# Attention stage: query weight pieces one after another, head norms woven between their halves, norm scratch in other tiles

## The chip, the cores and the metric

The kernel runs on one NeuronCore of one Trainium2 chip. The metric is the device time of one execution in microseconds (us). A core has TensorE (matmuls and transposes), VectorE (DVE in the rows), ScalarE (ACT), GpSimd (POOL) and SyncE (SP, which here only issues transfers). Each works through its own list of instructions in order, and they meet only at semaphores.

## The reference, cut to what matters

The whole reference is a sequence mixer with a table lookup, then a block of two layers over 256 tokens and 1024 channels: layer 0 pools and has a gated feed-forward net, layer 1 attends and has another one. The change lies in the attention of layer 1. Eight query heads of 128 share two key heads, and 256 context keys and values (worked out earlier) stand behind the 256 latent ones.

```python
q, k, v = split(h @ w_qkv)                 # 1024, 256, 256 columns
q = rmsnorm(q per head) * q_gain           # 8 heads
k = rmsnorm(k per head) * k_gain           # 2 key heads
q, k = rope(q), rope(k)                    # x * cos + swap(x) * sin
s = q @ keys.T * 128 ** -0.5
p = softmax(s)                             # fp32
o = p @ vals
x = x + gate * (o @ w_o)
```

## The kernel before, in words

**Layout.** Everything is kept turned, channels on the 128 partitions and the 256 tokens in the free dimension. `qT` holds the eight query heads, `kTt` the two key heads (latent columns 0 to 255, context 256 to 511).

**Weights in two parts.** A projection is worked out from a high and a low part of both operands, three matmuls of 256 columns instead of one (`mm3`, L1210). Weights come in pieces of 128x2048. For each piece ScalarE copies the high part (`hi_part`, L2547), VectorE (or GpSimd for pieces 34, 40 and 41) subtracts it to make the low part (`lo_part`, L1964), and only then can TensorE use it (`piece`, L1250). There are three places for the parts, so ScalarE may write piece n only when TensorE has used piece n - 3 (the wait on `p_u` n - 2). Piece 34 is the keys' weights, 35 the values', 36 to 39 the queries', two heads each, 40 to 43 the output projection's. A query piece is two halves (one head each) of 24 matmuls.

**Norm and rotation.** A `headnorm` n works on one key head (n = 0, 1; 256 columns) or on two query heads (n = 2 to 5; 512 columns). It is a chain that crosses the engines: ScalarE squares into a scratch tile (`square`), TensorE sums over the partitions by four matmuls with one column out ("hs"), ScalarE takes the root (`root`), VectorE the reciprocal, TensorE spreads it by four transposes ("hb"), VectorE multiplies head, gain and root ("hx"), TensorE swaps the rows for the rotation ("hr") while GpSimd multiplies by the cosine, VectorE multiplies the swapped rows by the sine ("ro"), and adds the two ("hn"). `scrs` has three sets of scratch, used in turn, so norm n's square waits for norm n - 3 to end.

**Order, written out by hand on each engine.** All engines' lists are Python loops and generators; `next(g)` puts down the next step of a generator.
- Pieces 34 and 35 (keys, values), then `colproj3` for pieces 36 and 37 (L1382).
- Norms 0 to 2 (two key heads and query heads 0 and 1), step by step over the three at once, with a step of `cond` after each. VectorE makes the low parts of pieces 38 and 39 only behind its third step of these norms (L2092), ScalarE the high parts behind its roots (L2623).
- `colproj3` for pieces 38 and 39, then the scores of head 0, norms 3 to 5 step by step with three more steps of `cond` and the scores of head 1.
- The loop over heads (L1400): transposes of the probabilities of head n, scores of head n + 2, output of head n - 1, and up to two steps of `cond`. `head_max` and `head_scale` are VectorE's side of the softmax, `exps` ScalarE's, `turned` the copies of the turned probabilities.

**cond** is `conditioning` (L788), which works out layer 1's modulation for the feed-forward net: 16 steps of four matmuls of 512 columns over eight 2 MB loads, some empty steps and two sums. Six steps lie ahead of the loop over heads, 18 calls in it.

**Loads.** SyncE issues 2 MB loads into three slots in turn; each waits until the slot's last content was used. In the attention the order is keys and values, two query loads, six `ada` loads for `cond`, the first half of the output weights, two `ada` loads, the second half, and then the feed-forward net's. A query load's slot is free when its second piece's low part is made (`split_done`), an `ada` load's when TensorE has used it.

**PSUM.** Eight banks, seven of them given out in turn by `take` (L651), which waits for the reader of what the bank held.

Of the kernel before, what the change touches and what calls it, by code (L numbers as in the profile page):

```python
# [96 lines left out]
def program(nc, a, out):  # L97
# [99 lines left out]
    def flat(ap):  # L197
        return ap.rearrange("p m n -> p (m n)")
# [166 lines left out]
    for l in range(2):  # L365
# [13 lines left out]
            (oT_[:, 0:512], oT_[:, 512:1024], oT_[:, 1024:1536]),  # L379
            (prT[:, 0:512], prT[:, 512:1024], prT[:, 1024:1536])]  # L380
# [267 lines left out]
    def _(pe):  # L648
# [693 lines left out]
        hn = [headnorm(0, kTt[:, 0, :], 1), headnorm(1, kTt[:, 1, :], 1)]  # L1342

        def colproj3(n0, name, reader, r0, per, base=None):

            for u in range(2):
                fresh = u == 0 and base is not None
                b = both_halves((name, u), reader, r0 + per * u, fresh)
                w = piece(n0 + u)
                for kk, i in rows_first(fresh):  # L1350
                    if fresh and i == 0:
                        row_there(base, kk)
                    k = mm3(b[i], both(w, 256 * kk + 128 * i, 128), both(ahx, 256 * kk, 256), kk == 0, kk == 7)
                k.then_inc(S["p_u"], 1)
# [26 lines left out]
        for q in range(2):  # L1381
            colproj3(36 + 2 * q, ("qp", q), "a_qT", 2 * q + 1, 1)  # L1382
            for u in range(2):
                hn.append(headnorm(2 + 2 * q + u, flat(qT[:, 4 * q + 2 * u:4 * q + 2 * u + 2, :]), 2))
            if q == 0:
                for _ in range(3):
                    for g in hn[0:3]:
                        next(g, None)
                    next(cond)
        hs = [head(h) for h in range(8)]  # L1390
        next(hs[0])
        rest = hn[3:]
        for s in range(3):
            for g in rest:
                next(g, None)
            if s == 1:
                next(hs[1])
            next(cond)
# [25 lines left out]
    def _(ve):  # L1424
# [638 lines left out]
        for u in range(2):  # L2063
            lo_part(36 + u, *half_piece(("q", 0), u))
        for _ in range(3):
            for g in hn[0:3]:
                next(g)
# [23 lines left out]

        for u in range(2):  # L2092
            lo_part(38 + u, *half_piece(("q", 1), u))
        for g in hn[0:3]:
            next(g)
        for step in range(4):
            for g in hn[3:6]:
                next(g)
            if step < 2:
                head_max(step)  # L2100
        for h in range(2):
            head_scale(h)
# [40 lines left out]
    def _(ac):  # L2143
# [459 lines left out]
        hi_part(37, *half_piece(("q", 0), 1))  # L2603
        ac.wait_ge(*at("p_vt", 1))
        told(copy(vt[:, 0, :], where["v", 0][:, 0:256]), "a_vt", 1)
        ac.wait_ge(*at("p_u", 36))
        told(copy(vt[:, 1, :], where["v", 1][:, 0:256]), "a_vt", 2)
# [13 lines left out]
        for q in range(2):  # L2621
            for u in range(2 * q):
                hi_part(38 + u, *half_piece(("q", 1), u))  # L2623
            for u in range(2):
                ac.wait_ge(*at("p_u", 37 + 2 * q + u))
                for i in range(2):
                    k = copy(qT[:, 4 * q + 2 * u + i, :], where[("qp", q), u][i])
                told(k, "a_qT", 2 * q + u + 1)
            if q == 0:
                for n in range(3):  # L2630
                    square(n)
                for n in range(3):
                    root(n)
        for n in range(3, 6):
            square(n)
        for n in range(3, 6):
            root(n)
# [28 lines left out]
        ac.wait_ge(*at("v_hn", 6))  # L2666
# [164 lines left out]
```

## Time and profile before

| | |
|---|---|
| median of 3 runs | 1692.29 us (1691.24 to 1695.68) |
| profiled execution, first to last instruction | 1707.0 us |
| instructions | 21947 |
| TensorE busy | 1486.5 us (87%) |
| VectorE busy | 1105.6 us (65%) |
| ScalarE busy | 583.2 us (34%) |
| GpSimd busy | 826.7 us (48%) |
| mean granted TensorE clock | 0.933 of full speed |

The profiled execution has no time of its own beside its span, so the span is what sums are made against. It is 14.7 us above the median of the runs. In a row of the timeline "1416.08 0.97" is the start and the duration in us; a duration covers a few instructions of one kind, and those of TensorE reach a little into the next row, so the time that a group of matmuls takes is read from its start to the next row's start. "[2.28 <-DVE wl L1439]" is idle time of the engine ahead of the row and what ended it. TensorE has two clock levels, 1.2 and 2.4 GHz, shown as 0.50 and 1.00.

### The profile page before, as it was taken

How to read it: one execution, taken by the hardware profiler on the slowest of the kernel's cores; microseconds unless marked ns; L12 is line 12 of the kernel's file. 1: busy time of each engine (PE TensorE's matmuls, PEld its weight loads, DVE VectorE, ACT ScalarE, POOL GpSimd, SP SyncE). 2: the span in 40 equal slices, each digit the busy share in tenths (PEclk: the TensorE clock that was granted, in tenths of full speed). 3: DMA queues.
4: the chain of work that ended last, by engine and by line, in shares of the span. 5: the costliest groups of instructions: out<-in, count | busy, mean ns of one | idle time of the engine just before them, and what ended most of it. 6: DMA issues, size and time to landing. Idle time of an engine off the chain costs nothing.

```text
span 1707.0 us, 21947 instructions
## 1 busy us (share of the span) xinstructions
PE 1486.5 (87%) x8188; PEld 1060.2 (62%) x8188; DVE 1105.6 (65%) x2161; ACT 583.2 (34%) x846; POOL 826.7 (48%) x746
## 2 busy tenths in 40 slices
PE   7999999756566799998878866889999999999999
PEld 6997675644222366664434421438998875689987
DVE  4855533797497877877756655227886535568865
ACT  6652341211121122222000011227664434466652
POOL 0025230467777766655767677533764100227750
PEclk9999999988788799999989988899999889999999
DMA  7437860698999999999999999994554525645551
GB/s 274 149 121 301 319 258 25 244 381 309 401 408 371 383 390 403 403 402 404 387 406 407 395 332 408 343 355 162 184 198 173 197 79 217 249 147 177 176 195 46
DMA packets 154251, 477.14 MB, mean 280 GB/s; under 512 B 10017, under 2 KB 12321, under 8 KB 150945
## 3 DMA queue, kind: packets, MB, share of 16 engines
q0 software_dynamic: 73728, 268.47, 40.6%
q1 hardware_dynamic: 80416, 207.27, 33.4%
q8 instruction: 65, 1.06, 0.3%
q14 instruction: 42, 0.34, 0.1%
HBM read 474.65 MB, written 1.05 MB: 279 GB/s over the span
## 4 chain that ended last, share of the span: by engine, by line
PE 57%; DVE 10%; DMA 9%; POOL 9%; issue 8%; ACT 2%; another core or an unknown queue 0%; ACTq 0%; DVEq 0%; POOLq 0%
PE ps L672 55%; POOL arena L2763 7%; DMA arena<-in_peer_v,cl 7%; DVE arena L1823 2%; POOL wring L2763 2%; PE ps L676 1%; DVE arena L1439 1%; DMA wring<-in_peer_v,cl 1%; DMA arena<-in_peer_u,arena 1%; DVE wring L1823 1%; DVE arena L1445 1%; ACT arena L2158 1%; DMA wring<-in_ada 0%; DVE arena L1442 0%
## 5 line engine op out<-in xcount | busy, mean ns | idle before, releaser
L672 PE MATMUL ps<-arena,wring 128*128 128x256 f32 (+2 forms) x2360 | 603.4, 494 | 115.1 <-DMA arena<-in_peer_v,cl 87.9
L672 PEld LDWEIGHTS ps<-arena,wring 128*128 128x128 f32 (+1 forms) x2360 | 333.2, 168 | 367.5 <-issue 167.3
L1823 DVE CUSTOM_DVE_ANT_0 arena<-arena 128x1024 f32<-128x1024 f32 x214 | 257.6, 1225 | 141.8 <-DMA arena<-in_peer_u,arena 98.6
L2763 POOL DMA_INDIRECT arena<-in_peer_u,arena x214 | 239.0, 1117 | 203.8 <-DVE arena L1781 76.5
L2763 POOL DMA_INDIRECT arena<-in_peer_v,cl x214 | 226.5, 1058 | 86.7 <-issue 59.9
L672 PE MATMUL ps<-hhl,wh 128*128 128x256 f32 (+1 forms) x1056 | 254.2, 324 | 3.9 <-DVE hhl L1445 3.9
L2158 ACT ACT_TABLE_LOAD x64 | 82.1, 1283 | 400.7 <-DVE arena L1823 180.5
L1439 DVE TENSOR_TENSOR wl<-wring,wh 128x2048 fp32r<-128x2048 f32 (+1 forms) x76 | 168.3, 2215 | 57.1 <-ACT wh L2161 55.2
L672 PE MATMUL ps<-hhl,wl 128*128 128x256 f32 x704 | 199.7, 284 | 0.0
L672 PEld LDWEIGHTS ps<-hhl,wh 128*128 128x128 f32 x1056 | 177.5, 192 | 21.4 <-issue 4.6
L2161 ACT ACTIVATE wh<-wring 128x2048 fp32r<-128x2048 f32 (+1 forms) x78 | 146.1, 1873 | 70.1 <-PE ps L672 68.3
L672 PE MATMUL ps<-ahl,wh 128*128 128x512 f32 (+1 forms) x496 | 166.0, 366 | 0.1
L2781 POOL TENSOR_TENSOR cvb<-cvb 128x256 f32<-128x256 f32 x44 | 120.1, 2731 | 83.2 <-ACT cvb L2158 83.2
L1445 DVE SCALAR_TENSOR_TENSOR cvb<-ps,vec,cvb 128x255 f32<-128x255 f32 x264 | 127.5, 483 | 38.3 <-ACT cvb L2158 19.0
L672 PEld LDWEIGHTS ps<-hhl,wl 128*128 128x128 f32 x704 | 135.4, 192 | 0.0
L2717 POOL TENSOR_TENSOR arena<-arena,cl 128x256 f32<-128x256 f32 x56 | 43.8, 782 | 160.6 <-PE ps L672 157.3
L672 PEld LDWEIGHTS ps<-arena 128*128 128x128 f32 (+1 forms) x708 | 86.4, 193 | 46.5 <-issue 26.1
L672 PE MATMUL ps<-arena 128*128 128x128 f32 (+4 forms) x708 | 99.3, 296 | 17.8 <-issue 6.7
L2158 ACT ACTIVATE cvb<-ps,vec 128x256 f32<-128x256 f32 x132 | 74.5, 565 | 107.2 <-PE ps L672 69.5
L2161 ACT ACTIVATE arena<-ps 128x512 f32<-128x512 f32 (+1 forms) x97 | 56.0, 577 | 147.1 <-PE ps L672 85.1
L672 PEld LDWEIGHTS ps<-ahl,wh 128*128 128x128 f32 x496 | 95.3, 192 | 15.9 <-issue 0.5
L672 PE MATMUL ps<-ahl,wl 128*128 128x256 f32 x352 | 98.7, 280 | 0.0
(256 smaller groups left out, 2027.7 us busy)
## 6 DMA issues: line engine op xcount, KB each, us to landing
wring<-in_ups SPq DMA_DIRECT2D x33, 2048.0 KB
wring<-in_ada SPq DMA_DIRECT2D x24, 2048.0 KB, 11.6
wring<-in_ffn_w_down SPq DMA_DIRECT2D x12, 2048.0 KB
wring<-in_w_in SPq DMA_DIRECT2D x8, 2048.0 KB
wring<-in_ffn_w_down SPq DMA_DIRECT2D x6, 1536.0 KB
wring<-in_peer_wq SPq DMA_DIRECT2D x4, 2048.0 KB
wring<-in_attn_w_qkv SPq DMA_DIRECT2D x4, 2048.0 KB
wring<-in_w_out SPq DMA_DIRECT2D x2, 2048.0 KB
```

The lines of the kernel that those rows point to most:

```text
L672: return pe.matmul(o, l, r, start=start, stop=stop)
L676: return pe.transpose(o, i, ident[0:n, 0:n])
L1439: return ve.tensor_tensor(o, x, y, op)
L1445: return ve.scalar_tensor_tensor(o, x, s, y, op0, op1)
L1823: ve.tensor_tensor_reduce(out=o, in0=o, in1=h2[:, t, :], scale=1.0, scalar=0.0, op0=MUL, op1=ADD, accum_out=dots[j % 2][:, k:k + 1]).then_ ...
L2158: return ac.activation(o, x, f, bias=bias, scale=scale, accum_out=accum)
L2161: return ac.activation(o, x, ACT.Copy)
L2717: k = po.tensor_tensor(OTs[l % 2][:, m:m + 2, :], AM[:, m:m + 2, :], bc(cl[:, o:o + 128], 2, 1), MUL)
L2763: po.indirect_dma_start(out=ring[n % NR], out_offset=None, in_=table, in_offset=bass.IndirectOffsetOnAxis(ap=which, axis=0)).then_inc(S[f" ...
L2781: seq(po.tensor_tensor(cv[:, 0, :], cv[:, 0, :], cv[:, 1, :], MUL))
```

## The change

Pieces 36 to 39 now follow each other on TensorE, and the steps of the norms, of `cond` and the first scores are put down between pieces and between the two halves of a piece. `colproj3` is no longer used for the queries: `query_pair` does one piece and stops after each half. ScalarE squares the key heads ahead of its next high part, and makes the high parts of pieces 38 and 39 ahead of the roots and behind the first square of a query pair. VectorE makes the low parts of 38 and 39 between the steps of norms 0 and 1. Norms 2 to 5 no longer run three at a time but one or two. The scores of heads 0 and 1 are asked for as soon as norm 2 is done. ScalarE puts down one small Exp behind the last root, and its wait for norm 5 ahead of the loop over heads goes. The second and third set of scratch move from `oT` and `prT` into `yo`, the last quarter of `sqb` and the buffer `cvb[1]`. The number of matmuls, of loads and of `cond` steps stays as it was, six of the latter ahead of the loop.

```diff
@@ -376,8 +376,8 @@
     kTt = kT_[:, :].rearrange("p (c n) -> p c n", c=2)
     vt = vt_[:, :].rearrange("p (t e) -> p t e", t=4)
     scrs = [(sqb_[:, 0:512], sqb_[:, 512:1024], sqb_[:, 1024:1536]),
-            (oT_[:, 0:512], oT_[:, 512:1024], oT_[:, 1024:1536]),
-            (prT[:, 0:512], prT[:, 512:1024], prT[:, 1024:1536])]
+            (yo_[:, 0:512], yo_[:, 512:1024], yo_[:, 1024:1536]),
+            (sqb_[:, 1536:2048], yo_[:, 1536:2048], cvb[1].rearrange("p i n -> p (i n)"))]
     yo = yo_[:, :].rearrange("p (t d) -> p t d", t=2)
     SC = 128 ** -0.5
 
@@ -1340,6 +1340,18 @@
             yield
 
         hn = [headnorm(0, kTt[:, 0, :], 1), headnorm(1, kTt[:, 1, :], 1)]
+        hn += [headnorm(2 + i, flat(qT[:, 2 * i:2 * i + 2, :]), 2) for i in range(4)]
+
+        def query_pair(i):
+
+            b = both_halves(("qp", i // 2, i % 2), "a_qT", i + 1, False)
+            w = piece(36 + i)
+            for half in range(2):
+                for kk in range(8):
+                    k = mm3(b[half], both(w, 256 * kk + 128 * half, 128), both(ahx, 256 * kk, 256), kk == 0, kk == 7)
+                if half == 1:
+                    k.then_inc(S["p_u"], 1)
+                yield
 
         def colproj3(n0, name, reader, r0, per, base=None):
 
@@ -1378,24 +1390,16 @@
             k.then_inc(S["p_o"], 1)
             yield
 
-        for q in range(2):
-            colproj3(36 + 2 * q, ("qp", q), "a_qT", 2 * q + 1, 1)
-            for u in range(2):
-                hn.append(headnorm(2 + 2 * q + u, flat(qT[:, 4 * q + 2 * u:4 * q + 2 * u + 2, :]), 2))
-            if q == 0:
-                for _ in range(3):
-                    for g in hn[0:3]:
-                        next(g, None)
-                    next(cond)
+        qp = [query_pair(i) for i in range(4)]
         hs = [head(h) for h in range(8)]
-        next(hs[0])
-        rest = hn[3:]
-        for s in range(3):
-            for g in rest:
-                next(g, None)
-            if s == 1:
-                next(hs[1])
-            next(cond)
+        for g in (hn[0], hn[1], cond,
+                  qp[0], qp[0], hn[0], hn[1], cond,
+                  qp[1], qp[1], hn[0], hn[1], hn[2], cond,
+                  qp[2], hn[2], hn[3],
+                  qp[2], cond, hn[2], hn[3],
+                  qp[3], hn[3], hn[4],
+                  qp[3], hs[0], hn[5], hn[4], hs[1], hn[5], hn[4], cond, cond, hn[5]):
+            next(g)
 
         for n in range(9):
             if n < 8:
@@ -2060,11 +2064,6 @@
             yield
 
         hn = [headnorm(n, *hn_of[n]) for n in range(6)]
-        for u in range(2):
-            lo_part(36 + u, *half_piece(("q", 0), u))
-        for _ in range(3):
-            for g in hn[0:3]:
-                next(g)
         def head_max(h):
             for t in range(2):
                 n = 2 * h + t
@@ -2089,17 +2088,26 @@
             PTb = prT[:, 1024 * (h % 2):1024 * (h % 2) + 1024].rearrange("p (j q) -> p j q", j=4)
             told(ve.tensor_copy(PTb[:, :, 128:256], quad(where["pt", 2 * h + 1])), "v_pT", h + 1)
 
+        def steps(*ns):
+            for n in ns:
+                next(hn[n])
+
         for u in range(2):
-            lo_part(38 + u, *half_piece(("q", 1), u))
-        for g in hn[0:3]:
-            next(g)
-        for step in range(4):
-            for g in hn[3:6]:
-                next(g)
-            if step < 2:
-                head_max(step)
-        for h in range(2):
-            head_scale(h)
+            lo_part(36 + u, *half_piece(("q", 0), u))
+        steps(0, 1)
+        lo_part(38, *half_piece(("q", 1), 0))
+        steps(0, 1)
+        lo_part(39, *half_piece(("q", 1), 1))
+        steps(0, 1, 0, 1)
+        steps(2, 2, 3, 2, 2, 3, 3, 3)
+        steps(4)
+        head_max(0)
+        steps(4, 5)
+        head_max(1)
+        head_scale(0)
+        steps(5, 4, 4)
+        head_scale(1)
+        steps(5, 5)
 
         cond = conditioning(range(GROUPS_EARLY, 6), 11)
         for _ in range(6):
@@ -2600,41 +2608,49 @@
         for hk in range(2):
             k = copy(kTt[:, hk, 0:256], where["k"][hk])
         told(k, "a_k", 1)
+        ac.wait_ge(*at("v_row", 8))
+        ac.wait_ge(*at("g_row", 8))
+
+        def square(n):
+            if n > 2:
+                ac.wait_ge(*at("v_hn", n - 2))
+            told(actf(scrs[n % 3][0], hn_of[n][0], ACT.Square), "a_hsq", n + 1)
+
+        def root(n):
+            ac.wait_ge(*at("p_hs", n + 1))
+            told(actf(st[:, 32 + 4 * (n % 3):36 + 4 * (n % 3)], where["hs", n][:, 0:4], ACT.Sqrt, bias=eps, scale=1.0 / 128),
+                 "a_hrs", n + 1)
+
+        def query_pair(i):
+            ac.wait_ge(*at("p_u", 37 + i))
+            for half in range(2):
+                k = copy(qT[:, 2 * i + half, :], where["qp", i // 2, i % 2][half])
+            told(k, "a_qT", i + 1)
+
+        square(0)
+        square(1)
         hi_part(37, *half_piece(("q", 0), 1))
         ac.wait_ge(*at("p_vt", 1))
         told(copy(vt[:, 0, :], where["v", 0][:, 0:256]), "a_vt", 1)
         ac.wait_ge(*at("p_u", 36))
         told(copy(vt[:, 1, :], where["v", 1][:, 0:256]), "a_vt", 2)
-        ac.wait_ge(*at("v_row", 8))
-        ac.wait_ge(*at("g_row", 8))
-
-        def square(n):
-            if n > 2:
-                ac.wait_ge(*at("v_hn", n - 2))
-            told(actf(scrs[n % 3][0], hn_of[n][0], ACT.Square), "a_hsq", n + 1)
-
-        def root(n):
-            ac.wait_ge(*at("p_hs", n + 1))
-            told(actf(st[:, 32 + 4 * (n % 3):36 + 4 * (n % 3)], where["hs", n][:, 0:4], ACT.Sqrt, bias=eps, scale=1.0 / 128),
-                 "a_hrs", n + 1)
-
-        for q in range(2):
-            for u in range(2 * q):
-                hi_part(38 + u, *half_piece(("q", 1), u))
-            for u in range(2):
-                ac.wait_ge(*at("p_u", 37 + 2 * q + u))
-                for i in range(2):
-                    k = copy(qT[:, 4 * q + 2 * u + i, :], where[("qp", q), u][i])
-                told(k, "a_qT", 2 * q + u + 1)
-            if q == 0:
-                for n in range(3):
-                    square(n)
-                for n in range(3):
-                    root(n)
-        for n in range(3, 6):
-            square(n)
-        for n in range(3, 6):
-            root(n)
+        hi_part(38, *half_piece(("q", 1), 0))
+        root(0)
+        root(1)
+        query_pair(0)
+        square(2)
+        hi_part(39, *half_piece(("q", 1), 1))
+        query_pair(1)
+        root(2)
+        square(3)
+        root(3)
+        query_pair(2)
+        square(4)
+        root(4)
+        query_pair(3)
+        square(5)
+        root(5)
+        seq(actf(st[:, 46:47], eps, ACT.Exp))
 
         def exps(h):
             for t in range(2):
@@ -2663,7 +2679,6 @@
         for _ in range(6):
             next(cond)
         row = row_hi(8, ahx, oT)
-        ac.wait_ge(*at("v_hn", 6))
         for n in range(9):
             if n < 8:
                 turned(n)
```

## Rows read from the trace of the kernel before

**Rows 1.** Windows: busy us of each engine (x instructions), granted clock, DMA.

```profile
1373.50:1385.20 11.70, 11.67 (x98) 11.46 (x96) 0.00 (x0) 1.04 (x3) 0.00 (x0) 1.00 0.48 179
1385.20:1401.30 16.10, 12.38 (x67) 7.48 (x67) 6.72 (x11) 7.15 (x10) 2.72 (x3) 0.79 0.00 1
1401.30:1414.40 13.10, 13.10 (x97) 13.10 (x98) 3.72 (x4) 0.66 (x2) 0.00 (x0) 0.87 0.75 296
1414.40:1434.30 19.90, 16.54 (x76) 8.28 (x75) 10.98 (x23) 7.73 (x17) 3.80 (x3) 0.83 0.41 147
```

**Rows 2.** The chain that ended last, from the bubble to the loop over heads.

```profile
1398.86 2.30 DVE wl L1439
...
1436.44 0.70 DVE prT L2090
...
1453.14 3.25 DVE pr L1442
...
1463.79 8.18 DMA wring<-in_ada
```

**Rows 3.** TensorE's timeline, 1401 to 1440: start, duration, line, operands, count, idle before.

```profile
1401.30 0.35 PE L672 MATMUL ps<-ahh,wh 128*128 128x256 f32 x1 [2.28 <-DVE wl L1439]
...
1414.37 1.88 PE L672 MATMUL ps<-kT,qT 128*128 128x512 f32 x4
1416.08 0.97 PE L672 MATMUL ps<-cbase,sqb 128*128 128x1 f32 x8
...
1418.77 1.42 PE L672 MATMUL ps<-wring,gt 128*32 128x512 f32 x8
...
1426.71 1.06 PE L672 MATMUL ps<-wring,gt 128*32 128x512 f32 x8
1427.71 2.84 PE L672 MATMUL ps<-qT,cbase 128*128 128x512 f32 x6
1430.48 1.06 PE L672 MATMUL ps<-wring,gt 128*32 128x512 f32 x8
1434.30 1.38 PE L676 MATMUL ps<-cbase,pr 128*128 128x128 f32 x8 [2.76 <-DVE pr L1442]
...
1439.18 1.09 PE L676 MATMUL ps<-cbase,pr 128*128 128x128 f32 x8
```

**Rows 4.** Windows of TensorE alone: busy us (x), granted clock, DMA.

```profile
1388.20:1395.20 7.00, 7.00 (x36) 0.53 0.01 2
1419.40:1426.00 6.60, 6.00 (x20) 0.50 0.74 273
1431.60:1434.20 2.60, 0.00 (x0) 1.00 0.68 189
```

**Rows 5.** Groups by line and shape, 1368 to 1442: busy us, mean ns, idle before.

```profile
L2161 ACT ACTIVATE wh<-wring 128x2048 fp32r<-128x2048 f32 x3 | 5.7, 1912 | 0.1
L2073 DVE TENSOR_REDUCE st<-ps 128x1 f32<-128x512 f32 x7 | 4.8, 691 | 1.6 <-PE ps L672 1.4
L1445 DVE SCALAR_TENSOR_TENSOR qT<-qT,vec,ps 128x512 f32<-128x512 f32 x4 | 3.0, 747 | 1.2 <-PE ps L676 0.9
L2158 ACT ACTIVATE pr<-ps,st 128x512 f32<-128x512 f32 x6 | 4.1, 687 | 6.7 <-DVE st L1442 6.6
L1442 DVE TENSOR_SCALAR pr<-pr,st 128x512 f32<-128x512 f32 x6 | 2.9, 487 | 0.2
L2161 ACT ACTIVATE qT<-ps 128x256 f32<-128x256 f32 x8 | 2.6, 381 | 30.1 <-PE ps L672 30.1
L2797 POOL TENSOR_TENSOR prT<-qT,cl 128x512 f32<-128x512 f32 x2 | 2.5, 1262 | 0.2
L2158 ACT ACT_TABLE_LOAD x1 | 1.3, 1283 | 1.3 <-DVE st L1442 1.3
L2158 ACT ACTIVATE sqb<-qT 128x512 f32<-128x512 f32 x1 | 0.6, 630 | 0.0
```

**Rows 6.** GpSimd's timeline: the low part of piece 40.

```profile
1451.54 4.55 POOL L2791 TENSOR_TENSOR wl<-wring,wh 128x2048 fp32r<-128x2048 f32 x1 [25.35 <-ACT wh L2161]
```

More of the change, by code:

```diff
@@ L2602, in _ @@
         told(k, "a_k", 1)
[L2603 to L2607, printed above, removed]
         ac.wait_ge(*at("v_row", 8))
@@ L2619, in root @@
                  "a_hrs", n + 1)
-        for q in range(2):
-            for u in range(2 * q):
-                hi_part(38 + u, *half_piece(("q", 1), u))
-            for u in range(2):
-                ac.wait_ge(*at("p_u", 37 + 2 * q + u))
-                for i in range(2):
-                    k = copy(qT[:, 4 * q + 2 * u + i, :], where[("qp", q), u][i])
-                told(k, "a_qT", 2 * q + u + 1)
-            if q == 0:
-                for n in range(3):
-                    square(n)
-                for n in range(3):
-                    root(n)
-        for n in range(3, 6):
-            square(n)
-        for n in range(3, 6):
-            root(n)
+        def query_pair(i):
[5 more added lines that the diff above has]
+        square(1)
+        hi_part(37, *half_piece(("q", 0), 1))
+        ac.wait_ge(*at("p_vt", 1))
+        told(copy(vt[:, 0, :], where["v", 0][:, 0:256]), "a_vt", 1)
+        ac.wait_ge(*at("p_u", 36))
+        told(copy(vt[:, 1, :], where["v", 1][:, 0:256]), "a_vt", 2)
+        hi_part(38, *half_piece(("q", 1), 0))
[15 more added lines that the diff above has]
+        seq(actf(st[:, 46:47], eps, ACT.Exp))
         def exps(h):
```

## The prediction

> **What bounds the kernel now.** I read the page first (TensorE is busy for 87% of the span), then the windows of the attention stage, then the chain that ended last, then each engine's timeline. The windows [rows 1] are to be read for TensorE's load: the query pieces 36 and 37 run densely at full clock in 11.7 us, the next 16.1 us hold only 12.4 us of work at a clock of 0.79, pieces 38 and 39 take 13.1 us at 0.87, and the 19.9 us up to the loop over heads again have idle time and a clock of 0.83. The chain [rows 2] says who sets the pace: it leaves TensorE for VectorE's low part of piece 38 (1398.86, 2.30 us), which stands behind three steps of the norms, and passes through VectorE again ahead of the loop (the copy of turned probabilities at 1436.44). TensorE's timeline [rows 3] has the idle times: 2.28 us until that low part is there, 2.76 us until head 0's probabilities are scaled. In the windows of the clock [rows 4] stands the third loss: twice, for about 7 us, TensorE was granted 0.50, which is 1.2 GHz. Ahead of the fall at 1388.2 it had idled and then run the sums of the norms (one column out), ahead of the one at 1419.4 it had run three such groups in a row (1416.08 to 1418.77, [rows 3]); the idle 2.6 us at 1431.6 left it at 1.00.
>
> So from 1373.5, where the values' piece ends, to 1434.3, where head 0's transposes begin, 60.8 us pass. Behind it the loop over heads follows with the same program before and after.
>
> **The change, part by part.** *TensorE.* The same instructions stand in another order. Their sum at full clock: four pieces are two times the first window of [rows 1] (98 matmuls in 11.7 us, so 96 in 11.5), 23.0. Six norm sums: 1416.08 to 1418.77 holds three, 0.90 each, 5.4. Six cond steps at 1.00 (1426.71 to 1427.71), 6.0. Four swaps of 512 columns: three in 1427.71 to 1430.48, 0.92 each, 3.7; two of half the width, 0.9. Six times four transposes: half of the 1.09 at 1439.18, less what reaches into the next row, 0.5 each, 3.0. Scores of heads 0 and 1: 1.71 each (1414.37 to 1416.08), 3.4. All [rows 3]. Sum 45.4 us. If TensorE never waits it comes to head 0's transposes at 1373.5 + 45.4 = 1418.9, which is 15.4 us earlier.
>
> *Does it wait?* I walked down each engine's new list. Low part 37 comes later, since two squares (0.63 each) go ahead of its high part: 1372.3 + 2.3 = 1374.7, wanted at about 1384. High part 38 (1.91, [rows 5]) can be made once the values are done, 1376.1; its low part ends at 1379.2 behind two short reciprocals, wanted at 1392.6. High part 39 must wait for piece 36 (1382.0), the copy of two queries (2 x 0.38) and a square: 1385.4, low part 1387.7, wanted at 1402. Each has 8 us or more to spare, so the 2.28 us stall goes and nothing takes its place. If a piece were late after all, all that is behind it on TensorE waits with it. Between two steps of one norm on TensorE there is now at least a half piece (2.9 us) or a similar load, while the answer (root and reciprocal of four columns, or a multiply of 0.75) takes about 1 us with its hand-overs. Only at the end is it tight. TensorE finishes the last half piece 9.2 us before the end of its sum (two scores 3.4, a sum 0.9, two groups of transposes 1.0, two swaps 1.8, two cond steps 2.0), at 1409.7. The last sum is wanted after head 0's scores, 1411.4, and its square is there at 1409.7 + 0.76 + 0.63 + 0.1 = 1411.2 [rows 5]: no loss, or a tenth.
>
> *VectorE's tail.* The last score of head 1 is there at 1414.5. From then it has to do: a maximum (0.69 and a short one behind it), 1415.4; two scalings of head 0 (0.49 and a short reciprocal ahead of each, 1.4 for both), 1416.8; hx of norm 5 (0.75), 1417.5; the sine part and the sum of norm 4 (passes over 512 columns as the maximum's, 0.7 each), 1419.0; head 1's scalings, 1420.4; sine part and sum of norm 5, 1421.9 [rows 5]. TensorE wants hx of norm 5 at 1418.0, so it doesn't wait for that. VectorE's first copy in the loop comes at 1421.9 in place of 1436.44 [rows 2], 14.5 us earlier. Before, the chain passed through VectorE there and stayed near it up to the scaling at 1453.14, so I take VectorE's 14.5 and not TensorE's 15.4. With six or so more hand-overs at below 0.1 us, 14.
>
> *The Exp behind the last root* takes the table load (1.28, [rows 5]) away from the first exponential. ScalarE gets to it at about 1412.8, loads until 1414.1, and the exponentials of head 0 (0.69, plus 0.1 for the sum read out) are there at 1415.1 and 1415.9, before VectorE wants them. The Trainium skill ("ScalarE: Activation LUTs", section "What ACT_TABLE_LOAD costs") gives 2.66 us for a switch of tables, a drain included, where the row has 1.28; by that the exponentials would come 1.4 us later, VectorE's tail would move by about 1 us, and the gain would be 13. No sum here uses that.
>
> *Scratch tiles.* Only addresses move. ScalarE's wait for norm 5 ahead of the loop falls away because its copies no longer overwrite scratch; by the walk norm 5 ends at 1421.9, while that engine's first copy can now go at 1420.1, and TensorE wants it only at about 1425, so this neither gains nor costs. GpSimd's products (1.26, [rows 5]) stand beside other work of VectorE.
>
> *Loads.* Piece 39's slot is free at 1387.7 and not 1403.5, so the third and fourth `ada` loads come some 16 us earlier, in time for cond steps at 1416. The fifth and sixth wait for TensorE's own cond steps and move with them. In the loop every load is released by a step of the loop: the last `ada` load, which the chain shows for 8.18 us up to 1471.97 [rows 2], starts when a cond step ends. It shifts with the loop.
>
> **Sum.** 1707.0 - 14 = 1693.0 for an execution as profiled; the median of the runs lies 14.7 us under the span, which I leave as it is, so 1692.3 - 14 = 1678.3 for the median. I say 1678.5.
>
> **The rivals.** *The clock falls once or twice in the new stretch.* The norm sums remain, and at 1373.5 two of them stand together, at the end one beside transposes. A spell as at 1388.2 lasts 7 us at half rate [rows 4] and costs 3.5 us where TensorE is the bound, less the 0.9 that it has over VectorE. One gives 1681, two 1685. For it: both spells of this stage followed such sums. Against it: three together before, now two at most with no idle time next to them, and 2.6 us of idle time that left the clock alone.
>
> *The tail hands over in single file.* Norms 4 and 5 share the last 9 us with scores, maxima and scalings on VectorE. If each of the five crossings there cost 1 us of TensorE's time, the gain is 9: 1683. GpSimd adds to it: a scaling of 0.49 took 3.25 us at 1453.14 [rows 2] while GpSimd made a low part for 4.55 us [rows 6], and ended with it. If the two new scaling pairs fall on GpSimd's products, each pair loses up to 1.26 us, so 2.5 at most. The Trainium skill ("GPSIMD Engine Reference", section "1. Specifications") names an SBUF interface shared with VectorE in its two-port mode. By the walk, though, the products end at about 1415.0 and 1419.2, just ahead of the scalings. The other way round, if the loop shifts so that the collision at 1453 is missed, 2.7 us more are won: with TensorE's 15.4 that makes 18, or 1674.
>
> *The gain is given back to loads.* Then the loop would start earlier and wait for its last two `ada` loads (8.2 us each) at their old times, and the total is 1692, no change. For it: the chain already has that load. Against it: its release is a cond step of the loop itself.
>
> *Slower: the clock stays low through the woven stretch.* All 45 us would be one mix of pieces and short groups in other banks. The third window of [rows 1] prices it: 13.1 us for what takes 11.5 at full clock, at a mean of 0.87, which is 3.4 us at half rate, so that 1.6 of 3.4 us were lost and slow work takes 1.9 times as long. The stretch would take 86 us, 41 more, and the kernel 1719. It decides from 16 us of the work on: run slow, that eats the 14; 21 us of it make the kernel slower by 0.3%. The Trainium skill ("TensorE: Matmul & The Clock Gate", section "A second HAM failure mode: psum-queue depth-cycling") reports a kernel in which going round the banks between groups made the clock go up and down. Against it in this trace: the loop over heads is such a mix, and the third window of [rows 4], at its edge, is at 1.00.
>
> **How the numbers follow.** The forecast (1675 to 1681) has a chance of 0.56, the clock falling once or twice 0.20, the single file 0.12, the loads 0.07, the slower one 0.05. The range reaches from 18 us gained, 1674, to 1685.5, the case of two spells; beyond lie the loads' case, the slower one and a little. A difference of 0.3% (5 us) is about what a measurement of this kernel can tell from none. Faster by more needs under 1687.2, which holds for the first three: 0.88. Within 0.3%: 0.07. Slower: 0.05.
>
> **What would show it.** In the profile after: no idle time of TensorE above 0.3 us between the values' piece and head 0's transposes, and about 45 to 46 us between them in place of 60.8; VectorE's low parts of 38 and 39 done long before their pieces; no wait of TensorE on `wl`; the table load ahead of the first maximum's use; a granted clock of 0.95 or more over the stretch. From the loop on, the same distances between rows as before, 14 us earlier. Wrong would be: a window at 0.50 among the query pieces, TensorE waiting for `sqb`, `yo` or `st` at the last two norms, or a longer wait for `in_ada`.

## The result and the profile after

The changed kernel takes 1687.35 us (median of 15 runs, 1681.92 to 1691.96) against 1692.29 us (15 runs, 1686.57 to 1699.67): a ratio of 0.9963, 95% interval 0.9951 to 0.9974. By the ratio it is faster by 6.3 us of 1692 (4.4 to 8.3), and the two medians lie 4.9 us apart; 14 were forecast, and 6.8 was the least that the range held (1685.5). The profiled execution spans 1684.7 us and took 1686.46.

The two spans, 1707.0 and 1684.7, lie 22 us apart, and most of that isn't the change's. VectorE's first row part of the attention (`ahl<-sqb`) starts at 1358.98 before and at 1342.47 after, 16.5 us earlier, in a stretch that the change doesn't touch; in the runs below, those with the old order among them, it starts anywhere from 1342 to 1352. So everything here is counted from that instruction, called S, over T (TensorE's first transposes of probabilities, where the loop over heads begins) and C (VectorE's first copy in the loop) to D (the last modulation values, `derived<-mods`, just ahead of the output projection).

The windows of the changed kernel, beside [rows 1]: the woven stretch, the first 21 us of the loop, and the two windows behind. The columns are the length, the busy time of TensorE, its weight loads, VectorE, ScalarE and GpSimd, then TensorE's granted clock and the transfers.

```profile
1357.10:1403.00 45.90, 45.61 (x335) 35.73 (x334) 21.38 (x37) 15.55 (x31) 6.23 (x6) 1.00 0.49 186
1403.00:1424.30 21.30, 21.30 (x117) 12.59 (x115) 18.64 (x42) 13.18 (x28) 3.00 (x2) 1.00 0.53 193
1424.30:1431.90 7.60, 0.03 (x2) 0.05 (x1) 7.33 (x4) 2.85 (x3) 7.00 (x3) 0.68 0.74 276
1431.90:1440.80 8.90, 8.90 (x33) 3.78 (x34) 4.10 (x10) 2.36 (x6) 0.19 (x1) 0.70 0.01 2
```

The first row is what the change was to do: where before 60.8 us held 53.7 us of TensorE's work at 0.79 to 1.00, now TensorE is busy for 45.6 of 45.9 us, at a granted clock of 1.00. The third row is new. For 7.6 us TensorE does nothing while VectorE is busy for 7.33 us with four instructions and GpSimd for 7.00 with three. In TensorE's timeline it stands between the two groups of head 4's transposes:

```profile
1402.97 1.04 PE L676 MATMUL ps<-cbase,pr 128*128 128x128 f32 x8
...
1423.65 0.66 PE L676 MATMUL ps<-cbase,pr 128*128 128x128 f32 x4
1431.88 1.09 PE L676 MATMUL ps<-cbase,pr 128*128 128x128 f32 x4 [7.58 <-DVE mods L1443]
1432.76 3.62 PE L672 MATMUL ps<-kT,qT 128*128 128x512 f32 x4
...
1449.43 1.07 PE L672 MATMUL ps<-wring,gt 128*32 128x512 f32 x8 [1.00 <-DMA wring<-in_ada]
```

The row before with that wait had 1.49 us at the same place (1457.47). The transposes' bank is given back by a small sum on VectorE (`mods`), and that stands behind head 5's two scalings. VectorE's timeline and GpSimd's show what those met:

```profile
1419.02 0.49 DVE L1446 TENSOR_SCALAR pr<-pr,st 128x512 f32<-128x512 f32 x1
...
1423.27 3.22 DVE L1446 TENSOR_SCALAR pr<-pr,st 128x512 f32<-128x512 f32 x1
1426.52 0.16 DVE L2081 RECIPROCAL st<-st 128x1 f32<-128x1 f32 x1
1426.72 4.79 DVE L1446 TENSOR_SCALAR pr<-pr,st 128x512 f32<-128x512 f32 x1
1431.54 0.19 DVE L1443 TENSOR_TENSOR mods<-ps,vec 128x32 f32<-128x32 f32 x1
```

```profile
1421.67 4.53 POOL L2806 TENSOR_TENSOR wl<-wring,wh 128x2048 fp32r<-128x2048 f32 x1 [18.30 <-ACT wh L2169]
1426.73 4.50 POOL L2806 TENSOR_TENSOR wl<-wring,wh 128x2048 fp32r<-128x2048 f32 x1 [0.52 <-ACT wh L2169]
```

Each scaling ends just under 0.3 us behind a low part of GpSimd: 1426.49 behind 1426.20, 1431.51 behind 1431.23. The first hold-up (3.22 us for 0.49) was in the kernel before too [rows 2, 6]. The second is new. Before, the second scaling began at 1456.61 and GpSimd's low part of piece 41 at 1457.41, so the scaling was through. Now they begin at 1426.72 and 1426.73, and it lasts 4.79 us. The two rows before:

```profile
1456.61 0.49 DVE L1442 TENSOR_SCALAR pr<-pr,st 128x512 f32<-128x512 f32 x1
```

```profile
1457.41 4.54 POOL L2791 TENSOR_TENSOR wl<-wring,wh 128x2048 fp32r<-128x2048 f32 x1 [1.32 <-ACT wh L2161]
```

The long idle time then costs once more, since TensorE's clock falls during it (window of TensorE alone, 0.50 is 1.2 GHz):

```profile
1427.60:1437.10 9.50, 5.22 (x12) 0.50 0.30 124
```

5.22 us of that is work, which at full clock would have been about half. Idle time 7.6 - 1.5 = 6.1, and 2.6 for the clock, make 8.7; T to D grew from 47.45 to 56.21 us, by 8.8. (The kernel before went through its loop at 1.00 in its profile, behind the 1.49 us too.)

### The profile page after: what moved, and what is told of

The parts are those of the page before. It is cut to its first block, busy times and chain, and to the rows that moved or that the text cites. A ratio compares the mean times of both kernels' runs of the same rounds, so it can differ in the third digit from the quotient of the medians.

```text
span 1684.7 us, 21948 instructions
## 1 busy us (share of the span) xinstructions
PE 1473.1 (87%) x8188; PEld 1055.2 (63%) x8188; DVE 1109.2 (66%) x2161; ACT 583.6 (35%) x847; POOL 827.5 (49%) x746
## 4 chain that ended last, share of the span: by engine, by line
PE 55%; DVE 13%; DMA 10%; POOL 10%; issue 5%; ACT 2%; DVEq 0%; ACTq 0%; POOLq 0%
PE ps L672 53%; POOL arena L2778 8%; DMA arena<-in_peer_v,cl 6%; DVE arena L1827 3%; DMA arena<-in_peer_u,arena 2%; POOL wring L2778 2%; PE ps L676 2%; DVE arena L1443 1%; DVE arena L1449 1%; DMA wring<-in_peer_v,cl 1%; DVE wring L1827 1%; DVE pr L1446 1%; DMA wring<-in_peer_u,arena 1%; ACT arena L2166 1%; DMA wring<-in_ada 1%
## 5 line engine op out<-in xcount | busy, mean ns | idle before, releaser
L672 PE MATMUL ps<-arena,wring 128*128 128x256 f32 (+2 forms) x2360 | 592.0, 486 | 105.3 <-DMA arena<-in_peer_v,cl 99.6
L2778 POOL DMA_INDIRECT arena<-in_peer_u,arena x214 | 244.4, 1142 | 187.5 <-DVE arena L1785 77.4
L672 PE MATMUL ps<-arena 128*128 128x128 f32 (+4 forms) x708 | 99.3, 296 | 20.5 <-ACT arena L2169 11.7
```

Of the source, the lines that this page charges most:

```text
L672: return pe.matmul(o, l, r, start=start, stop=stop)
L2778: po.indirect_dma_start(out=ring[n % NR], out_offset=None, in_=table, in_offset=bass.IndirectOffsetOnAxis(ap=which, axis=0)).then_inc(S[f" ...
```

## The experiments

Theory A: the two low parts of the output weights on GpSimd hold up head 5's scalings, and that takes away more than half of what the woven stretch gives. Theory B: the scalings are only what the trace shows on its chain, and the end of the loop is set by the last `ada` load (8.57 us on the chain after, 8.18 before), so the gain would be lost anyway. By its interval a run's ratio is uncertain by 2 to 4 us; S to T and T to D come from one profile each. The profile before was 1.5 us longer from S to T than the other two with the same program up to T (e6, e9), so every gain in the column of S to D holds about 1.5 us that belong to that one profile.

| kernel | S to T, us | T to D, us | S to D against before | ratio, 95% interval |
|---|---|---|---|---|
| before | 75.32 | 47.45 | | 1 |
| changed | 60.50 | 56.21 | -6.1 | 0.9963, 0.9951 to 0.9974 |
| e1_wait | 60.27 | 51.84 | -10.7 | 0.9944, 0.9928 to 0.9959 |
| e2_nudge | 60.59 | 50.35 | -11.8 | 0.9937, 0.9924 to 0.995 |
| e3_quarters | 60.09 | 49.49 | -13.2 | 0.9949, 0.9936 to 0.9963 |
| e4_short | 60.63 | 46.23 | -15.9 | 0.9918, 0.9899 to 0.9938 |
| e5_act_scale | 60.74 | 45.78 | -16.3 | 0.9906, 0.9882 to 0.993 |
| e6_before_early | 73.75 | 55.26 | +6.2 | 1.004, 1.0023 to 1.0058 |
| e7_parts_only | 69.82 | 48.42 | -4.5 | 0.9964, 0.9951 to 0.9978 |
| e8_no_exp | 59.78 | 55.65 | -7.3 | 0.9952, 0.9932 to 0.9972 |
| e9_before_act | 73.88 | 47.27 | -1.6 | 0.999, 0.9976 to 1.0003 |
| e10_after_again | 59.97 | 55.65 | -7.2 | 0.9956, 0.994 to 0.9971 |

**e1_wait.** GpSimd's second low part waits until head 5 is scaled.

```diff
         for u in range(2):
+            if u == 1:
+                po.wait_ge(*at("v_p", 12))
             lo_part(40 + u, *half_piece(("o", 0), u))
```

> The changed kernel, with GpSimd waiting for head 5's second scaling before it makes the low part of piece 41. Theory A (GpSimd's low part 41 holds up VectorE's second scaling of head 5, 4.79 us for 0.49, TensorE idles 7.6 us and its clock falls): the second scaling takes 0.5 us again, the first still 3.2 us; TensorE idles about 3 us there, no 10 us spell at 0.50; total 5 to 8 us under the changed kernel, so 1680 to 1682 and a ratio to the kernel before of 0.993 to 0.994. Theory B (the last ada load, 8.57 us on the chain, ends the loop over heads at its own time): the collision goes but the total moves by less than 1.5 us, 1686 to 1688.

GpSimd's low part 41 began at 1429.95, with 1.14 us of waiting for the scaling, and only one slow scaling is left:

```profile
1425.89 3.21 DVE L1446 TENSOR_SCALAR pr<-pr,st 128x512 f32<-128x512 f32 x1
```

TensorE idled 3.27 us at the place of the 7.58, and then ran at 0.50 for 5.8 us (window 1430.20 to 1436.00). T to D fell by 4.4 us, the ratio to 0.9944, 3.2 us under the changed kernel's. That is less than the 5 to 8 of theory A and more than B allows; the two intervals of the ratios still overlap, so the profile carries this verdict.

**e2_nudge.** Work that serves nothing is added, so that GpSimd starts later.

```diff
             if n in (2, 3):
+                if n == 3:
+                    for i in range(2):
+                        seq(copy(yo_[:, 512 * i:512 * i + 512], kTt[:, i, :]))
                 hi_part(38 + n, *half_piece(("o", 0), n - 2))
```

> The changed kernel, with two copies of 128x512 (0.6 us each, work that serves nothing) on ScalarE ahead of the high part of piece 41, so that GpSimd's low part begins about 1.3 us later. Theory A (a race for 0.01 us): the second scaling of head 5 gets in first and takes 0.5 us, adding work makes the kernel faster by 4 to 7 us, 1680 to 1683. Theory B: no change, or up to 1 us slower, 1687 to 1688. A third, that the scaling is slow whatever GpSimd does there: the second scaling stays above 4 us.

Measured 1682.84 us, ratio 0.9937, 4.4 us under the changed kernel's: two useless copies make it faster. VectorE's timeline has the second scaling back at 0.49 us:

```profile
1427.00 3.21 DVE L1446 TENSOR_SCALAR pr<-pr,st 128x512 f32<-128x512 f32 x1
1430.24 0.16 DVE L2081 RECIPROCAL st<-st 128x1 f32<-128x1 f32 x1
1430.44 0.49 DVE L1446 TENSOR_SCALAR pr<-pr,st 128x512 f32<-128x512 f32 x1
```

The loss isn't all gone, though: T to D is 50.35 us, 2.9 more than before, with the same one slow scaling. TensorE now waits 3.27 us for it, where it waited 1.49 before:

```profile
1431.30 1.09 PE L676 MATMUL ps<-cbase,pr 128*128 128x128 f32 x4 [3.27 <-DVE mods L1443]
```

Behind that wait the clock is 0.70 over 5 us (window 1431.30 to 1436.30), where the kernel before had 1.00.

**e3_quarters.** GpSimd makes each of the two low parts in four instructions.

```diff
+            if n > 34:
+                for i in range(3):
+                    seq(po.tensor_tensor(lo[:, 2 * i:2 * i + 2, :].bitcast(FR), src[:, 2 * i:2 * i + 2, :],
+                                         hi[:, 2 * i:2 * i + 2, :], SUB))
+                hi, lo, src = (x[:, 6:8, :] for x in (hi, lo, src))
             told(po.tensor_tensor(lo.bitcast(FR), src, hi, SUB), *split_done(n))
```

> The changed kernel, with GpSimd's low parts of pieces 40 and 41 made in four instructions of 128x512 each. Theory A: a scaling can be held up by one quarter at most, about 1.2 us in place of 3.2 and 4.8, so TensorE idles 1 to 3 us and the total is 6 to 9 us under the changed kernel, 1678 to 1681. Theory B: under 1.5 us of change. If a held-up VectorE doesn't get in between two GpSimd instructions, the scalings stay at 3 us or more.

The longest scalings are now 1.3 us, so VectorE does get in between two instructions of GpSimd:

```profile
1432.37 1.31 DVE L1446 TENSOR_SCALAR pr<-pr,st 128x512 f32<-128x512 f32 x1
...
1433.92 1.18 DVE L1446 TENSOR_SCALAR pr<-pr,st 128x512 f32<-128x512 f32 x1
```

T to D fell by 6.7 us in the profile. The total fell only by 2.4 (0.9949) where 6 to 9 were expected, within the intervals of no gain at all over the changed kernel. Profile and total differ here by more than in any other run: S to D gives 13.2 us, or 11.7 without the 1.5 of the profile before, and the ratio 8.6, give or take 2.3. How much of that is noise I can't say.

**e4_short.** GpSimd works out only 16 of 256 columns of the two low parts, and the rest is left out.

```diff
+            if n > 34:
+                hi, lo, src = (x[:, 0:8, 0:16] for x in (hi, lo, src))
```

> The changed kernel, with GpSimd working out only a sixteenth of the low parts of pieces 40 and 41 (16 of 256 columns; the rest is left out). Theory A: all scalings take 0.5 us, and the total shows what the collisions cost in all, 8 to 12 us under the changed kernel, 1675 to 1679; the 13 to 14 us that the walk gave up to the loop over heads then reach the end, with 2.7 more for the collision of the kernel before. Part of that can come from the output weights' second load, which starts earlier here. Theory B: the total stays within 2 us of 1687.

No scaling is slow, T to D is 46.23 us, the ratio 0.9918: 7.6 us under the changed kernel's, just under the 8 to 12 expected. The last `ada` load is on the chain for 8.14 us here as well, so it has moved with the loop. Theory B is out. Of this run's gain a part may be the output weights' second load, which can start earlier here; e5 has no such doubt.

**e5_act_scale.** ScalarE scales heads 5 and 6, with VectorE making the reciprocals. Nothing is left out. ScalarE's side (VectorE leaves out these four scalings, and TensorE waits for ScalarE's):

```diff
+            if h in (5, 6):
+                for n in range(2 * h, 2 * h + 2):
+                    P_ = pr[:, 512 * (n % 4):512 * (n % 4) + 512]
+                    ac.wait_ge(*at("v_rp", n - 9))
+                    told(actf(P_, P_, ACT.Copy, scale=st[:, 8 * (n % 4) + 3:8 * (n % 4) + 4]), "a_ps", n - 9)
```

> The changed kernel, with the scalings of heads 5 and 6 done by ScalarE (VectorE only makes their reciprocals), all else as it is. If what costs the time is the scalings of these two heads being held up by GpSimd's low parts, no scaling is held up, since ScalarE took 0.6 us for such a pass elsewhere, and from the first copy of the loop to the end of the loop it takes 42 to 44 us, as with a sixteenth of the low parts (42.3), against 52.3 in the changed kernel; total 8 to 11 us under the changed kernel's ratio of 0.9963, so a ratio of 0.990 to 0.992, about 1677 to 1680. If ScalarE is held up as well, or it becomes the bound, the loop stays above 46 us and the ratio above 0.994.

1679.09 us, ratio 0.9906, 9.6 us under the changed kernel's. C to D is 41.90 us. ScalarE scales beside GpSimd's low part 40 (1425.55 to 1430.09) and isn't held up to speak of: 0.72 us each, two in 1.48 us, where a square of that size took it 0.63 [rows 5]. The window of the loop has TensorE nearly full at a clock of 1.00.

```profile
1427.69 1.48 ACT L2173 ACTIVATE pr<-pr,st 128x512 f32<-128x512 f32 x2
```

```profile
1406.00:1452.60 46.60, 45.84 (x254) 26.83 (x255) 30.03 (x66) 28.71 (x57) 12.76 (x7) 1.00 0.74 273
```

**e6_before_early.** The other side of the race, in the kernel before.

```diff
+            if n == 3:
+                hi_part(41, *half_piece(("o", 0), 1))
             if n > 0:
                 out_head(n - 1)
                 row(n - 1)
-            if n in (2, 3):
+            if n == 2:
```

> The kernel before, with one step of ScalarE put elsewhere: the high part of piece 41 goes ahead of the copy and row of head 2's output instead of behind them, about 1 us earlier. Theory A (a race between head 5's second scaling and GpSimd's low part 41): the low part now begins at the end of the one of piece 40, ahead of that scaling, which takes 4 us or more; TensorE idles 6 us or more and its clock falls; 4 to 8 us slower than the kernel before, 1696 to 1701, ratio 1.0025 to 1.0045. Theory B (the loss is bound to the new order of the norms, not to this race): no change, ratio 0.999 to 1.001.

1701.77 us, ratio 1.004. GpSimd made both low parts without a pause (9.20 us from 1438.46), the second scaling took 4.40 us, TensorE idled 5.07 us in place of 1.49, and T to D was 55.26. With not one instruction of the norms moved, the kernel before loses most of what the changed kernel loses: 6.8 us by the ratio, 7.8 by T to D. The copy and the row of head 2's output come some 2 us later on ScalarE by this edit, but TensorE shows no wait for them.

```profile
1440.06 3.25 DVE L1442 TENSOR_SCALAR pr<-pr,st 128x512 f32<-128x512 f32 x1
...
1443.54 4.40 DVE L1442 TENSOR_SCALAR pr<-pr,st 128x512 f32<-128x512 f32 x1
```

**e7_parts_only.** One part of the change alone: high and low part of pieces 38 and 39 are made early, while TensorE keeps its order. VectorE's side (its old place behind the norms goes, and ScalarE's high parts are moved in the same way):

```diff
         for u in range(2):
             lo_part(36 + u, *half_piece(("q", 0), u))
+        for u in range(2):
+            lo_part(38 + u, *half_piece(("q", 1), u))
         for _ in range(3):
             for g in hn[0:3]:
                 next(g)
```

> The kernel before, with one part of the change: high and low part of pieces 38 and 39 are made early, as the changed kernel does it, while TensorE keeps its order (norms 0 to 2 step by step between the piece pairs). If the walk is right, this takes away the idle 2.3 us ahead of piece 38 and at most the short spell of half clock behind it (1.6 us), while the steps of the norms stay bare: 2 to 4 us less up to the first copy of the loop (77.5 us from the first row part to it, so 73.5 to 75.5), and a total 2 to 4 us lower if the race at head 5 stays won. If instead the late low part was the cause of the whole bubble, the way to the loop shrinks by 10 us or more.

S to T is 69.82 us, 4.1 to 5.5 less than in the three kernels with the old order, so a little over the 2 to 4 expected. TensorE goes from the norms into piece 38 with no wait, and the short spell at half clock behind the idle time is gone (window 1380.00 to 1393.20, clock 1.00). The ratio of 0.9964 is as good as the whole change's, since the race stays won. It makes 6.1 us (3.7 to 8.3), more than the 2 to 4 expected; the profile (S to D, less the 1.5 us) shows 3.0, so part of it isn't accounted for.

**e8_no_exp.** The small Exp is left out.

> The changed kernel without the small Exp behind the last root. The first maximum is there before ScalarE is done with the last root, so the table load starts at the same moment with or without it: no change beyond 0.3 us up to the loop, ratio 0.995 to 0.998. If the Exp is what took the load off the chain, the way to the loop grows by 1.3 us.

ScalarE loads the table right behind the last root either way, since the first maximum is already there:

```profile
1397.57 0.26 ACT L2166 ACTIVATE st<-ps,st 128x4 f32<-128x4 f32 x1 [1.20 <-PE ps L672]
1397.85 1.28 ACT L2166 ACT_TABLE_LOAD   x1
1399.15 0.69 ACT L2166 ACTIVATE pr<-ps,st 128x512 f32<-128x512 f32 x1
```

No difference to be told in the total (0.9952), and S to T isn't longer. The Exp gives nothing.

**e9_before_act and e10_after_again.** The edit of e5 on the kernel before, and the changed kernel once more.

> The kernel before, with the scalings of heads 5 and 6 on ScalarE, as in the run that did the same to the changed kernel (ratio 0.9906). If the order of the norms is worth its 13 us by itself and the races are apart from it, this gains only the 2.7 us and 0.7 us by which the two scalings of the kernel before were held up: loop over heads 41.5 to 43 us in place of 45.3, ratio 0.9975 to 0.9985, about 1688 to 1690. The two kernels without races then lie 12 to 14 us apart. If moving the scalings is worth more for its own sake, this gains 6 us or more.

> The changed kernel once more, with nothing edited, on the same chip as the kernel before with its scalings moved, so that the two can be compared. If the race is lost in every execution: second scaling of head 5 above 4 us again, loop over heads 52 us, ratio 0.995 to 0.9975. If it is lost only in some: a profile with a second scaling of 0.5 us and a loop of about 45 us.

e9 has no slow scaling, and yet a loop as long as before, 47.27 us against 47.45, and a ratio of 0.999, which can't be told from 1. The two loops aren't alike in clock, though. Behind the same 2.76 us of idle time ahead of the loop, e9 was granted 0.54 over its first 3.65 us, e6 0.57 and e7 0.58, and the profile of the kernel before 1.00. The windows from T to D of e9, its first 3.65 us, and T to D of the kernel before and of e5:

```profile
1416.35:1463.62 47.27, 46.52 (x252) 27.71 (x253) 27.46 (x64) 28.74 (x57) 11.55 (x6) 0.96 0.69 259
1416.35:1420.00 3.65, 3.65 (x11) 2.63 (x12) 2.62 (x7) 0.60 (x1) 0.00 (x0) 0.54 0.95 408
```

```profile
1434.30:1481.75 47.45, 45.30 (x252) 26.56 (x253) 30.98 (x68) 25.85 (x53) 11.53 (x6) 1.00 0.69 258
```

```profile
1406.84:1452.62 45.78, 45.02 (x253) 26.54 (x252) 29.22 (x65) 28.73 (x57) 11.94 (x7) 1.00 0.74 277
```

Against e7, which also enters at half clock and has the hold-up (48.42), e9 is 1.15 us shorter; by the ratio it gains 1.7. So being held up for 2.7 us at the first scaling cost the old order one to two us, and my expectation of 2.3 to 3.8 in the loop was too high. With both races out, the two orders differ by 0.999 - 0.9906 = 0.84%, 14.2 us (within about 5, by the two intervals). e10 lost the race again (4.79 us from 1430.19, GpSimd from 1430.20), as did e8: three profiles of three with this loop.

## Why the prediction was wrong

**The bubble and the woven stretch: right, with the sum 0.5 us short.** 45.4 us were worked out, 45.9 measured. TensorE waited once, 0.18 us. The clock stayed at 1.00, so the spells of [rows 4] are gone and neither clock rival came; going round the banks between groups, with which the Trainium skill explains the clock's ups and downs in another kernel ("TensorE: Matmul & The Clock Gate", section "A second HAM failure mode: psum-queue depth-cycling"), didn't lower it here. S to T is 60.3 us on average of eight profiles, against 75.32, 73.75 and 73.88 with the old order, so the gain up to T is 14.0 and not 15.4: the profile before was itself 1.5 us longer there than its two likes. e7 puts 4 to 5.5 us of it down to the early weight parts, and the rest to the weaving.

**VectorE's tail: 0.9 us longer than worked out.** C comes 3.87 us behind T, where the walk had 3.0 (1421.9 and 1418.9). Part of it is one more collision: the sum of norm 4 took 1.21 us for 0.69 beside GpSimd's product for norm 5 (1402.09 to 1403.37). TensorE waited for none of it here; what VectorE's lag costs comes further down the loop.

**The step that failed: "From the loop on, the same distances between rows as before, 14 us earlier."** I had worked out two different shifts for the loop, 15.4 us for TensorE and 14.5 for VectorE, and then let everything in the loop move by one. Measured, the distance from T to C grew by 1.7 us (2.14 to 3.87), and it was paid twice.

First, in the race. ScalarE's high part of piece 41 stands behind the copy of an output of TensorE, the scalings stand in VectorE's list. Before, ScalarE waited 0.84 us for that output and made the high part 2.22 us after head 5's first scaling began (1455.36 and 1453.14); now it didn't wait and made it 1.41 us after (1424.68 and 1423.27). ScalarE before, and after:

```profile
1454.49 0.38 ACT L2161 ACTIVATE oT<-ps 128x256 f32<-128x256 f32 x1 [0.84 <-PE ps L672]
1454.91 0.42 ACT L2158 ACTIVATE ahh<-oT 128x256 fp32r<-128x256 f32 x1
1455.36 1.91 ACT L2161 ACTIVATE wh<-wring 128x2048 fp32r<-128x2048 f32 x1
```

```profile
1423.81 0.39 ACT L2169 ACTIVATE oT<-ps 128x256 f32<-128x256 f32 x1
1424.23 0.42 ACT L2166 ACTIVATE ahh<-oT 128x256 fp32r<-128x256 f32 x1
1424.68 1.91 ACT L2169 ACTIVATE wh<-wring 128x2048 fp32r<-128x2048 f32 x1
```

The lead of the scaling over GpSimd's low part was 0.80 us, and all but 0.01 of it went. The second scaling then took 4.79 us. e2 moves this one start by 1.3 us and takes 5.9 of the 8.8 us away; e6 moves it by as much the other way and brings the loss into the kernel before.

Second, at the first scaling. It is held up for the same 2.7 us in both orders, but TensorE comes to that place 1.7 us earlier against VectorE, so it waits 3.27 us (e1, e2) where it waited 1.49, and its clock falls behind the longer wait. That is the 2.9 us by which e2 is still longer than the kernel before from T to D: 1.7 of idle time and 1.2 because the work went slower (TensorE is busy for 46.51 us against 45.30). Against e5, where this hold-up is gone too, it is 50.35 - 45.78 = 4.6 us.

That the two scalings cost the time is shown by the runs. That TensorE's lead over VectorE brought it about is read from the rows (it grew by 1.73 us, the wait at the first scaling by 1.78): no run moves TensorE alone against VectorE.

I had the mechanism in hand, and priced it in the wrong place: the new scaling pairs beside GpSimd's products at up to 1.26 us each (neither met one, as the walk had it: they start 1.1 and 0.8 us behind a product's end), and the pair at 1453 only as a thing that could go away. Its worst case is the length of a low part, 4.5 us, and the fall of the clock behind the idle time.

**Size of the loss.** Against the same kernel without any hold-up (e5) T to D is 10.4 us longer: 7.6 us of idle time and 2.6 for the clock. Against the kernel before it is 8.8, and 14.0 - 8.8 = 5.2 is what the total shows within its interval (6.3). With the new hold-up alone gone (e2) the ratio gives 0.9937 x 1692.29 = 1681.6 us, in the range but 3 above the forecast of 1678.5; with both gone (e5) 0.9906 x 1692.29 = 1676, under it. So the gain up to T was forecast nearly rightly (14.0 for 15.4), and what of it reaches the end hangs on these two scalings.

**The other rivals.** The loads didn't take the gain: in every run the last `ada` load lies 8.1 to 8.6 us on the chain, wherever the loop is. The slower case didn't come. One ground against the clock rivals was luck of a single profile: that 2.76 us of idle time ahead of the loop left the clock at 1.00 held for the kernel before, and in e6, e7 and e9, with the same wait, it then stood at 0.54 to 0.58.

**The Exp:** worked out as taking the load off the chain, it does nothing (e8). ScalarE reaches it after the maximum is there. The row shows 1.28 us between root and exponential and no drain beside it, so the 2.66 us of the Trainium skill ("ScalarE: Activation LUTs", section "What ACT_TABLE_LOAD costs") didn't arise here.

**What stays open.** Why e3's total is some us worse than its profile, and e7's better. Why the old order's loop was entered at full clock in one profile and at half clock in three. What that does is known: without slow scalings T to D is 45.8 us in the new order and 47.3 in the old, TensorE idles for 0.75 us in both, and it is busy for 45.02 us at 1.00 (e5) against 46.52 at 0.96 (e9), so the clock is the whole of the 1.5 us.

## What to carry to other kernels

When a change moves two engines by different amounts, work out every place downstream where a long instruction of one starts near a short one of the other, and price it by the long one, not by what the old trace happened to show. A lead of under a microsecond is not a lead. A hold-up that was there before isn't free for that: it grows when the engine that waits for it comes earlier. Short work that a whole loop waits for is best put on an engine that the long work beside it doesn't hold up: here the scalings on ScalarE are worth 9.6 us in the new order, more than the reordering itself gained by the total, and 1.7 us, not clear of noise, in the old.

## What the runs showed of the hardware

A fast pass of VectorE over SBUF (128x512, 0.49 us) that met a low part of GpSimd ended just under 0.3 us behind it, wherever in it the pass began: it took 3.22 and 4.79 us beside low parts of 4.5 us, 1.2 to 1.3 us beside quarters of about 1.3. It was so even where both started within 0.01 us (after, e8, e10). The Trainium skill ("GPSIMD Engine Reference", section "1. Specifications") names contention of VectorE's two-port modes and of its instructions with two SBUF inputs; the first agrees with these rows, and the second with the 1.21 us for 0.69. Passes that read PSUM weren't held up: in the kernel before a maximum over 128x512 took its usual 0.69 us at 1459.06, in the middle of low part 41. And from S to T the same program took 73.75, 73.88 and 75.32 us in three profiles, so a stage from a single profile was good to 1.5 us here and no better. TensorE's clock differed as well: behind the same 2.76 us of TensorE's idle time it was granted 1.00 in one profile, and 0.54 to 0.58 over the next 3.7 to 3.9 us in three.
